# Gated recurrence in a two-block transformer stack: forget factors multiplied level by level in place of exponentials of summed logarithms

## The reference, cut to what matters

```
logf = log_sigmoid(z) + log1p(lb * exp(-z))          # z: forget pre-activation, lb: lower bound per channel
k    = (1 - lb) * sigmoid(-z)                        # f = lb + (1-lb) sigmoid(z);  k = 1 - f
# S_t = diag(f_t) S_{t-1} + k_t v_t^T ;  o_t = S_t^T q_t
b     = cumsum(logf)
decay = exp(min(b[t] - b[s], 0)) * (s <= t)
A[t,s] = sum_d q[t,d] * decay[t,s,d] * k[s,d]
o      = A @ v    (+ the part across chunks)
o      = o * rsqrt(mean(o*o) + eps) * out_g
```

## Time and profile before

| | |
|---|---|
| median of 3 runs | 1033.12 us |
| span of the profiled execution (first to last instruction) | 1031.7 us |
| TensorE matmul busy | 1019.3 us (99%) |
| VectorE busy | 730.5 us (71%) |
| ScalarE busy | 654.4 us (63%) |
| GpSimd busy | 11.3 us (1%) |
| mean granted clock of TensorE | 0.998 |
| chain that ended last | TensorE 86%, ScalarE 5%, VectorE 4%, DMA 3% |

### The profile page before, as it was taken

The page is one execution under the profiler, slowest core; times in us unless marked ns, Lnnn a source line. Parts: engine busy times, 40 slices in busy tenths (PEclk is TensorE's granted clock), DMA queues, the critical chain, the costliest instruction groups (busy, mean ns, idle before and its releaser), DMA issues.

```text
span 1031.7 us, 19279 instructions
## 1 busy us (share of the span) xinstructions
PE 1019.3 (99%) x8170; PEld 912.9 (88%) x8170; DVE 730.5 (71%) x1070; ACT 654.4 (63%) x911; POOL 11.3 (1%) x15
## 2 busy tenths in 40 slices
PE   9999999999999999999999999999999999999997
PEld 7899987888989999988999998888799999988875
DVE  5774688875656888765565657978875656699686
ACT  7677667564465565644466678767755657676683
POOL 0000000000000000000000000100000000001000
PEclk9999999999999999999999999999999999999999
DMA  8852454476547655566554543423665455344231
GB/s 292 300 195 83 144 164 145 161 232 207 174 153 232 187 164 188 191 216 189 168 159 122 174 143 109 157 84 104 192 199 167 134 163 164 101 140 149 84 105 61
DMA packets 97431, 167.54 MB, mean 162 GB/s; under 512 B 6913, under 2 KB 32257, under 8 KB 96833
## 3 DMA queue, kind: packets, MB, share of 16 engines
q1 hardware_dynamic: 95792, 159.18, 48.7%
q0 software_dynamic: 1120, 5.51, 1.5%
q10 hardware_dynamic: 432, 1.62, 0.4%
HBM read 165.23 MB, written 1.05 MB: 161 GB/s over the span
## 4 chain that ended last, share of the span: by engine, by line
PE 86%; ACT 5%; DVE 4%; DMA 3%; issue 2%; SPq 0%; DVEq 0%; ACTq 0%
PE proj L625 13%; PE proj L627 12%; PE proj L626 12%; PE proj L634 12%; PE proj L636 12%; PE proj L635 12%; DMA raw<-in_w_in 2%; DVE wlo L1587 1%; DMA raw<-in_w_mem_kv 1%; ACT whi L1110 1%; PE mix L955 1%; PE mix L956 1%; PE mix L695 1%; PE mix L987 1%; PE mix L670 1%
## 5 line engine op out<-in xcount | busy, mean ns | idle before, releaser
L1587 DVE TENSOR_TENSOR wlo<-raw,whi 128x1024 fp32r<-128x1024 f32 (+2 forms) x304 | 355.0, 1199 | 140.2 <-ACT whi L1110 138.3
L1110 ACT ACTIVATE whi<-raw 128x1024 fp32r<-128x1024 f32 (+2 forms) x304 | 305.8, 1038 | 147.8 <-PE proj L636 63.3
L625 PE MATMUL proj<-act_hi,whi 128*128 128x256 f32 x1064 | 303.5, 285 | 0.9 <-ACT arena L1388 0.5
L627 PE MATMUL proj<-act_hi,wlo 128*128 128x256 f32 x1064 | 301.0, 283 | 0.0
L626 PE MATMUL proj<-act_lo,whi 128*128 128x256 f32 x1064 | 300.9, 283 | 0.0
L625 PEld LDWEIGHTS proj<-act_hi,whi 128*128 128x128 f32 x1064 | 203.1, 191 | 3.9 <-ACT arena L1388 1.4
L626 PEld LDWEIGHTS proj<-act_lo,whi 128*128 128x128 f32 x1064 | 203.2, 191 | 0.9
L627 PEld LDWEIGHTS proj<-act_hi,wlo 128*128 128x128 f32 x1064 | 203.2, 191 | 0.2
L634 PE MATMUL proj<-whi,y_hi 128*128 128x512 f32 (+1 forms) x340 | 134.9, 397 | 0.8 <-DVE y_lo L2099 0.4
L635 PE MATMUL proj<-wlo,y_hi 128*128 128x512 f32 (+1 forms) x340 | 131.7, 387 | 0.0
L636 PE MATMUL proj<-whi,y_lo 128*128 128x512 f32 (+1 forms) x340 | 131.7, 387 | 0.0
(11 more groups left out here) (360 smaller groups left out, 1232.7 us busy)
## 6 DMA issues: line engine op xcount, KB each, us to landing
raw<-in_w_in SPq DMA_DIRECT2D x144, 512.0 KB, 4.5
raw<-in_w_up SPq DMA_DIRECT2D x88, 256.0 KB, 4.3
raw<-in_w_out SPq DMA_DIRECT2D x32, 512.0 KB, 4.2
raw<-in_w_down SPq DMA_DIRECT2D x22, 512.0 KB, 4.8
raw<-in_w_mem_k SPq DMA_DIRECT2D x8, 512.0 KB, 4.1
raw<-in_w_o SPq DMA_DIRECT2D x8, 512.0 KB, 4.0
raw<-in_w_mem_v SPq DMA_DIRECT2D x8, 512.0 KB, 4.3
raw<-in_w_mem_kv SPq DMA_DIRECT2D x7, 512.0 KB, 6.4
```

The costliest lines, as they stand in the source:

```text
L625: mm(o, wh[:, i, wc], hi[:, k0 + i, :], start=begin and j % 2 == 0, stop=False, skip_group_check=True)
L627: last = mm(o, wl[:, i, wc], hi[:, k0 + i, :], start=False, stop=end, skip_group_check=True)
L1110: fn(whi[c % SPLIT][:, 0:w], raw[c % SLOTS][:, 0:w], ACT.Copy).then_inc(s.w_hi, 1)
L1587: tt(wlo[c % SPLIT][:, 0:w], raw[c % SLOTS][:, 0:w], f32(whi[c % SPLIT][:, 0:w]), ALU.subtract).then_inc(s.w_lo, 1)
```

## The change

The table `tree`, its load, the logarithm sums, the transposes and the exponentials go. The forget factor itself is made once (`FORGET`; layer 0: an exponential, layer 1: two exponentials and a multiply-add with the lower bound). Keys and queries of all 8 heads are then scaled in place, level by level from the smallest: `grow(half, four)` multiplies each 2*half block's keys in the left half and queries in the right half by the neighbouring block's total factor; `totals` multiplies totals pairwise for the next level. TensorE makes the products of one level for all heads (`products(l)`, l = 8 the diagonal, 7 the smallest blocks, 0 the top). Each `grow` waits for the level's products, since it overwrites their operands, and the next level's products wait for it. The copies out of PSUM for the three top levels move to ScalarE (`leave_32`, `leave_64`, `leave_128`). Outputs, squares and norms of all four pairs come at the end; `hgo` is one group in place of three, behind `mlaout1`.

```diff
-    groups[at:] = [("mlaout0", mlaout[0]), ("hgo0", []), ("hgg0", hg["hgg0"]), ("hgo1", []), ("hgg1", hg["hgg1"]), ("hgo2", []),
-                   ("mlaout1", mlaout[1])]
+    groups[at:] = [("mlaout0", mlaout[0]), ("hgg0", hg["hgg0"]), ("hgg1", hg["hgg1"]), ("mlaout1", mlaout[1]), ("hgo", [])]
 # TensorE
-                pe.wait_ge(s.hg_f, L + 1)
-                turn_logs(0)
...
+                products(8)
+                products(7)
                 pe.wait_ge(*stage(4, L))
                 project("mlaout0", L, y_hi, y_lo, 8, part=(1, 2))
-                decays(0, 2, 4)
+                products(6)
                 project("hgi1", L, act_hi, act_lo, part=(3, 4))
+                gates(0)
+                products(5)
+                gates(1)
+                products(4)
+                gates(2)
+                gates(3)
+                products(3)
+                gates(4)
+                products(2)
+                gates(5)
+                products(1)
+                gates(6)
+                gates(7)
+                products(0)
...
+                for p in range(4):
+                    outputs_within(p)
+                for p in range(4):
+                    outputs_across(p)
+                project("mlaout1", L, y_hi, y_lo, 8, part=(0, 1))
+                squares(0)
+                squares(1)
                 project("mlaout1", L, y_hi, y_lo, 8, part=(1, 2))
                 squares(2)
-                outputs(3)
-                project("hgout0", L, y_hi, y_lo, ready=y_ready, part=(0, 1))
                 squares(3)
-                project("hgout0", L, y_hi, y_lo, ready=y_ready, part=(1, 3))
+                project("hgout0", L, y_hi, y_lo, ready=y_ready, part=(0, 3))
 # ScalarE
+                    fn(HF, HF, ACT.Exp)
+                    fn(HT, HT, ACT.Exp).then_inc(s.hg_s, 1)
+                else:
+                    fn(FORGET, HT, ACT.Exp).then_inc(s.hg_f, 1)
...
+                for p in range(4):
+                    square(p)
                 split_until(ahead_of("mlaout1", L, 0))
+                logs(0)
+                logs(1)
+                roots(0)
+                split_until(ahead_of("mlaout1", L, 1))
                 rounded(0)
+                rounded(1)
+                nc.scalar.preload_act_table(ACT.Ln)
+                logs(2)
+                logs(3)
+                split_until(ahead_of("hgout0", L, 0))
+                roots(2)
 # VectorE
+                def grow(half, four):
+                    n = HALVES[::-1].index(half)
+                    dve.wait_ge(s.hg_pr, 18 * L + 2 * n + four + 3)
+                    if half > 1:
+                        dve.wait_ge(s.hg_g, 6 * L + n)
+                    z, across = sides(half, four)
+                    tt(z, z, across, ALU.mult).then_inc(s.hg_z, 1)
...
+                for half, l, name, n in ((1, 7, "mlaout0", 1), (2, 6, "hgi1", 3), (4, 5, "hgg0", 0), (8, 4, "hgg0", 1),
+                                         (16, 3, "hgg0", 3), (32, 2, "hgg1", 0), (64, 1, "hgg1", 1)):
+                    for four in range(2):
+                        grow(half, four)
+                    if half == 1:
+                        masked(8)
+                    if l >= 3:
+                        masked(l)
+                    if half < 32:
+                        totals(4 * half)
+                    if half == 4:
+                        dve.wait_ge(*done("mlaout0", L))
+                        tt(X[:, :, 0:512], bank("mlaout0", L), X[:, :, 0:512], ALU.add).then_inc(out_of("mlaout0", L)[0], 1)
+                    split_until(ahead_of(name, L, n))
+                    if half == 16:
+                        diagonal()
...
+                scaled(0)
+                scaled(1)
                 lower(0)
+                split_until(ahead_of("mlaout1", L, 1))
+                lower(1)
+                scaled(2)
+                scaled(3)
                 dve.wait_ge(*done("mlaout1", L))
                 tt(X[:, :, 512:1024], bank("mlaout1", L), X[:, :, 512:1024], ALU.add).then_inc(out_of("mlaout1", L)[0], 1)
+                split_until(ahead_of("hgout0", L, 0))
                 lower(2)
-                split_until(ahead_of("hgout0", L, 0))
-                scaled(3)
                 lower(3)
```

More of the change, by code:

```diff
@@ L1042, in outputs, with outputs_across @@
+                def outputs_across(p):
+                    pe.wait_ge(s.hg_ca, 6 * L + 5 + p // 2)
+                    for hd in range(2):
+                        h, o = 2 * p + hd, pair_bank(p)[:, hd * SEQ:(hd + 1) * SEQ]
+                        last = mm(o[:, P:SEQ], HV[:, 0, h * P:(h + 1) * P], AT[:, h, P:SEQ], start=False, stop=True, skip_group_check=True)
                     last.then_inc(s.hg_o, 1)
@@ new lines, in layer @@
+                products(5)
[11 more added lines that the diff above has]
+                products(0)
+                for half in range(2):
+                    pe.wait_ge(*out_of(f"hgi{half}", L))
+                pe.wait_ge(s.hg_at, L + 1)
+                pe.wait_ge(s.hg_ca, 6 * L + 4)
@@ new lines, in leave_32, with leave_64 @@
+                def leave_32():
+                    act.wait_ge(s.hg_zero, L + 1)
+                    act.wait_ge(s.hg_pr, 18 * L + 14)
+                    for n in range(2):
+                        rows = slice(64 * n, 64 * n + 32)
+                        src = mix[rows, LEVEL_BANK[2], :].rearrange("p (h b t) -> p h b t", h=HG_H, b=NB)
+                        fn(both(AT[rows, :, 64 * n + 32:64 * n + 64], HG_H, 32), src, ACT.Copy).then_inc(s.hg_ca, 1)
+                def leave_64():
+                    for four in range(2):
+                        act.wait_ge(s.hg_pr, 18 * L + 15 + four)
+                        src = mix[0:64, four, :].rearrange("p (h b t) -> p h b t", h=4, b=NB)
+                        fn(both(AT[0:64, 4 * four:4 * four + 4, 64:P], 4, 64), src, ACT.Copy).then_inc(s.hg_ca, 1)
@@ L2075, in diagonal @@
-                def diagonal(p):
-                    heads = slice(2 * p, 2 * p + 2)
-                    dve.wait_ge(s.hg_cp, 8 * L + 2 * p + 2)
-                    for j in range(4):
-                        rows = slice(32 * j, 32 * j + 32)
-                        last = copy(both(AT[rows, heads, 32 * j:32 * j + 32], SEQ, 32), AC[rows, 4 * p:4 * p + 4, :].rearrange("p (h b) t -> p h b t", b=2))
-                    last.then_inc(s.hg_at, 1)
+                dve.wait_ge(s.hg_f, L + 1)
+                dve.wait_ge(s.mla_g, 2 * L + 2)
@@ L2084, in gated @@
+                dve.wait_ge(*out_of("hgq1", L))
+                for four in range(2):
+                    h = slice(4 * four, 4 * four + 4)
+                    tt(HQP[:, h, :], HQT[:, h, :], FORGET[:, h, :], ALU.mult).then_inc(s.hg_z, 1)
+                latent_lower(1, s.mixed)
+                split_until(ahead_of("hgi0", L, 3))
+                totals(2)
+                split_until(ahead_of("hgi1", L, 1))
                 def gated(p):
                     dve.wait_ge(s.hg_sq, 4 * L + p + 1)
-                    o = bank(f"hgo{p}", L)[:, 0, :] if p < 3 else mix[:, 0, :]
+                    o = bank("hgo", L)[:, p, :] if p < 2 else mix[:, p - 2, :]
@@ L2126, in layer @@
+                split_until(ahead_of("hgg1", L, 3))
+                for half in range(2):
+                    dve.wait_ge(*out_of(f"hgg{half}", L))
+                gated(0)
+                gated(1)
+                dve.wait_ge(s.hg_w, 4 * L + 2)
+                nc.vector.memset(stat[:, 240:241], 0.0).then_inc(out_of("hgo", L)[0], 1)
+                split_until(ahead_of("mlaout1", L, 0))
                 gated(2)
+                gated(3)
                 scaled(0)
-                diagonal(3)
+                scaled(1)
```

484 lines of the change are left out of this document (156 added, 328 removed).

## The result

The changed kernel takes 1035.95 us (median of 16 runs, 1033.01 to 1040.25), the kernel before beside it 1033.43 us (16 runs, 1032.69 to 1036.34). The ratio is 1.0023 [1.0012, 1.0034]: 2.4 us slower, where 2.8 us faster was forecast. The time lies in the range, on the other side of no change. The spread has grown, 7 us against 4. The profiled execution is the slowest of the 16, span 1038.5 us and 1040.25 us in all; over the 16, time and granted clock roughly go together, from 0.987 (1034.05 to 1034.57 us) to 0.980 (1040.25 us). Every ratio is of fast executions: two of the kernel before beside the experiments, of 1430.87 and 3564.07 us, are left out.

A forecast was written before the change was run, and what follows sets the result against it. TensorE's unbroken row of matmuls was taken as the bound; 35.2 us removed, less 2 x 3.1, 2 x 9.3, 2 x 2.7 and 2.2, left 2.8 us gained: 1030.3 us, range 1023.5 to 1036.5.

The forecast's parts named there:

- where the end would stand and for how long: Before hgout0, TensorE waits 9.3 us a layer for mlaout1's PSUM tensor, released by VectorE's addition to X.
- What would be left without the bank: At the end, without the PSUM tensor's wait, TensorE would still wait some 4.5 us later on, for lower(2).
- The masked copy: VectorE's 512-column masked copy in the first levels: 0.68 us, 0.6 in a row; bounds 0.4 and 1.2.
- rival (c): Level ladder: dearer masked copies or `grow` make every level late, 5 us, 1035.5 us; chance 0.22.
- Rival (b): Waits don't form, end wait under 5 us, no fall of the clock: 1015 to 1020 us; chance 0.08.
- the clock at the end: After the end wait TensorE starts at the lower clock, costing 2.7 us a layer, between 0 and 3.5.
- rival (a): Clock does not fall in the end wait or is back at once: 5.4 us less, 1024.9; chance 0.14.
- the work removed: On TensorE, logarithm sums and transposes go, 33.2 us in both layers; fewer round trips, 0.6 in both.
- Wait 1: At the first levels TensorE waits for VectorE's masked copies and `grow`: 3.1 us a layer.
- 2.2 more: Layer 1: TensorE waits for shares, last keys, a late-split piece and the first `grow`, 2.2 us extra.
- a gain of 1.4 us: TensorE's waits at L987, said to stand behind unit-wise masked copies, go too: 1.4 us.
- a sign of being wrong: Named signs: an end wait under 5 us, `grow` over 1.3 us, or TensorE busy above 98%.

The follow-up runs named there:

- experiment 1: Changed kernel with the group hgo ahead of mlaout1 in the order of the PSUM tensors: 1029.9 us, ratio 0.9964 to the kernel before.
- experiment 2: Changed kernel with 19 unused float32 matmuls put ahead of hgout0, inside the end wait: 1033.59 us, ratio 0.9991 to the kernel before.
- experiment 7: The seventh kernel: experiment 6 with the small levels also set apart by projection pieces as in experiment 3: 1008.83 us, ratio 0.9747 to the kernel before.
- experiment 4: Changed kernel with grow(1) done one side at a time, keys and queries by themselves: 1035.19 us, ratio 1.0008 to the kernel before.
- experiment 6: Changed kernel with hgo ahead of mlaout1, grow(1) by side, and the end reordered on three engines: 1010.69 us, ratio 0.9764 to the kernel before.
- experiment 9: Changed kernel with ten more small float32 matmuls ahead of layer 0's level products: 1036.72 us in its one execution.
- experiment 5: Changed kernel with the diagonal products (level 8) left out, two single small matmuls standing for them: 1036.54 us, ratio 1.0021 to the kernel before.
- experiment 3: Changed kernel with a projection piece between levels 8 and 7, 7 and 6, 6 and 5: 1033.56 us, ratio 0.9995 to the kernel before.
- experiment 8: Kernel before with the small matmuls issued twice in three of four odd units a layer: 1068.26 us, ratio 1.0314 to the kernel before.

## Why the prediction was wrong, step by step

**Right: where the end would stand and for how long.** The chain was read from the order on three engines and priced from the earlier trace rows: 9.3 us forecast, 9.31 and 9.31 measured, by the same releaser. What would be left without the bank was 4.5 forecast, 5.4 measured (experiment 1). The masked copy was 0.68 forecast, 0.73 measured, so the ladder of rival (c) did not come about as priced: its time, 1035.5 us, is close to the measured one, but the trace shows 0.3 us of waits for `grow`. That nearness is luck. Rival (b) is out by the 18.6 us.

**Right in kind, too high: the clock at the end.** 2.7 us a layer was taken from the earlier trace rows; the matmul distances give 1.6 and 2.2, and experiment 2 agrees with their sum. That it falls at all, against rival (a), the windows show (0.50).

**About right: the work removed.** The seventh kernel has the same 8042 matmuls at a clock of 0.997 and is busy for 987.7 us: 31.6 less than the earlier trace rows, against 33.2 and 0.6 by the sum.

**Wrong: the first levels, in two terms.** Wait 1 was 3.1 us a layer, from VectorE's list alone, and layer 1 had 2.2 more. Measured are 9.1 us of `issue` gaps in this execution, the slowest, and 5.6 to 6.6 in those of experiments 1, 2, 4, 6 and 9, whose levels stand in the same order; of waits for `grow` 0.3. The prediction had the sign before it: the earlier trace rows has two `issue` waits on L987, the small matmuls' line, and counted them as a gain of 1.4 us on the ground that they stood behind masked copies. Those two ended 1.4 us after an instruction packet had landed, like all the others. The change keeps these matmuls, 1536 records on L951 as on L987, and sets two bursts side by side; the cause grew where the sum let it go. And `grow(1)` was priced at 1.14 us because a form at the earlier trace rows costs the same at all block sizes; it took 2.1, over the 1.3 that the prediction itself had named as a sign of being wrong. Its waits came out only when the gaps were gone (7.8 us in experiment 5, 2.4 of them for the matmuls left out there), so gaps and waits stand in one place and the prediction priced one of the two.

**Missing: the clock in the first levels.** The same 8042 matmuls are busy for 997.3 us in the changed kernel and 987.7 in the seventh: 9.6 us more, 5.4 forecast. By the distances of the matmuls 3.8 are at the two ends and 1.6 in the first block, at 178.6 us, which the change doesn't touch; some 4 are left for the levels, where none was forecast and the windows show 0.83.

**Missing: 1.1 us a layer** at L616 for ScalarE's evacuation (L1081). Before, the group `hgo0` stood between `hgi1` and the gates; now the gates need `hgi1`'s tensor two groups on, and `gates(0)` follows its last piece at once. This was read from the order of the groups, no run tried it.

**The account.** Idle time has grown by 28.8 us where 25.6 was forecast (18.6 + 6.2 + 2.2 - 1.4). That these are near each other is partly luck: the end wait is the forecast one, but 11.3 us of gaps and of waits for ScalarE stand where 8.4 us of waits for `grow` and layer 1's keys were forecast. Busy time has fallen by 22.0 where 28.4 was (33.8 - 5.4). That is 3.2 + 6.4 = 9.6 us, and the span is 6.8 us longer where 2.8 shorter was forecast. Typical runs lie 4 us below this one, so the typical miss is 5.2 us. The length of the gaps, the falls of the clock behind them and the fall in the first block, which all differ from execution to execution, are the likely causes of the spread; how much of it belongs to each is not shown.

**Open:** why a packet sets off 2.7 us before TensorE stops at one boundary and 1.0 after at another, or early enough for no gap at all. The DMA share of the stretch does not decide it: there are gaps in windows with DMA shares of 0.36 and 0.39, and none in the window of experiment 7 with 0.81.

## What to carry to other kernels

Count instructions for each stretch, not only matmul time: many tiny float32 matmuls in a row can outrun the supply of instructions (256 in 1.22 us here), and an "issue" entry in a profile is a reason not to put more of the same work beside it. Spreading it out was worth about 2.9 us here (experiment 3), no more, because other waits lay beneath. Before a group's position in a rotation of buffers is changed, ask whose evacuation it will wait for and what stands ahead of that evacuation; here one such wait was forecast to a tenth and was still worth 27 us, with the order behind it and the slow first `grow`, once it was taken out. Waits that lie over each other hide each other, so a single repair that gains nothing (experiment 5) doesn't acquit the cost it removed.

## What the runs showed of the hardware

- TensorE's instructions come in packets of 16384 bytes, some 256 instructions. Where 256 go by in 1.22 us TensorE can stand for 0.2 to 3.3 us at a packet's end, and it goes on 1.26 to 1.58 us after the next packet has landed (50 gaps in eleven traces). The Trainium skill, "Runtime: NRT & Kernel Launch", section "Instruction fetch mechanics", gives blocks of 16 KiB with 256 instructions, and the trace agrees; of crossing from one to the next it says that this is mostly hidden. It was so at all but 5 of the 63 packets here and not in the bursts, whose gaps were 9.1 us here and 16.6 in experiment 8.
- The granted clock fell not only in a wait of 9 us: in two windows with gaps of 2.08 and 1.88 us among small matmuls it was 0.83. After the end wait it was back 3.6 us (layer 0) and 4.8 us (layer 1) after the first matmul, at a cost of 1.6 and 2.2 us. With TensorE kept at work in the wait it stayed at 1.00.
- A 128x1024 product of VectorE whose neighbouring elements lie in two far regions took 2.1 us, where the same form with other strides takes 1.2; the same as two products of 128x512, each in one region, 1.4 us. A masked copy of 128x512 took 0.73 us.
